# Column blocks of the mixer's input matrix in another order

## The reference, cut to what matters

```python
z = rms(x) @ w_in                     # 1024 x 2304: nine blocks of 256 columns
y_pool = pool_mix(z[:, 0:256])        # block 0: sums over 2, 4, 8, 16 tokens, then a small product
h = z[:, 256:512] * sigmoid(z[:, 512:768])          # blocks 1 and 2
y_conv = silu(layer_norm(depthwise_conv(h, 31))) @ pw_w + pw_b
q = rope(rms(z[:, 768:1280]) * g_q)   # blocks 3, 4: four heads of 128
k = rope(rms(z[:, 1280:1792]) * g_k)  # blocks 5, 6
v = z[:, 1792:2304]                   # blocks 7, 8
y_att = attention(q, k, v)            # prompt: causal; samples: two cached pages of keys and values each
x = x + concat(y_pool, y_conv, y_att) @ w_out
```

## Time and profile before

| | before |
|---|---|
| median of three runs | 1561.97 us |
| profiled execution | 1565.14 us |
| its span, first to last instruction | 1563.6 us |
| PE busy in the span | 1470.0 us (94%) |
| DVE busy in the span | 973.2 us (62%) |
| mean granted clock of TensorE | 0.972 |
| mixer stage, first layer | 137.8 us |
| mixer stage, second layer | 133.9 us |

### The profile page before, as it was taken

The page is one execution under the profiler, slowest core; times in us unless marked ns, Lnnn a source line. Parts: engine busy times, 40 slices in busy tenths (PEclk is TensorE's granted clock), DMA queues, the critical chain, the costliest instruction groups (busy, mean ns, idle before and its releaser), DMA issues. The chain is left out here.

```text
span 1563.6 us, 30270 instructions
## 1 busy us (share of the span) xinstructions
PE 1470.0 (94%) x11110; PEld 1386.0 (89%) x11110; DVE 973.2 (62%) x1366; ACT 594.1 (38%) x827; POOL 125.6 (8%) x167
## 2 busy tenths in 40 slices
PE   5999999968999999999989999997899998999998
PEld 4999999746978799999989999995688787999997
DVE  4766546886745467665466664578756554766643
ACT  4333344233534244333353333441445332433331
POOL 3000000342001110000000000006220110000000
PEclk7999999989999999999999999998999999999999
DMA  7566455326548647655456655552474666555552
GB/s 225 163 168 167 156 173 162 108 89 223 178 149 285 243 133 207 165 161 166 132 146 171 166 162 165 159 162 68 151 247 136 221 213 236 141 166 166 170 163 91
DMA packets 310010, 263.95 MB, mean 169 GB/s; under 512 B 7096, under 2 KB 292024, under 8 KB 309882
## 3 DMA queue, kind: packets, MB, share of 16 engines
q1 hardware_dynamic: 290242, 203.14, 43.3%
q0 software_dynamic: 13776, 48.97, 8.8%
q10 hardware_dynamic: 5896, 10.54, 2.2%
HBM read 254.65 MB, written 8.56 MB: 168 GB/s over the span
## 5 line engine op out<-in xcount | busy, mean ns | idle before, releaser
L1330 PE MATMUL pairs<-h_hi,w_hi 128*128 128x288 f32 x1824 | 545.5, 299 | 14.8 <-DVE h_lo L863 10.6
L1330 PE MATMUL pairs<-h_hi,w_lo 128*128 128x288 f32 x1824 | 544.2, 298 | 0.0
L1330 PE MATMUL pairs<-h_lo,w_hi 128*128 128x288 f32 x1824 | 543.9, 298 | 0.0
L860 DVE TENSOR_TENSOR w_lo<-raw_weights,w_hi 128x1024 fp32r<-128x1024 f32 (+1 forms) x388 | 450.3, 1202 | 135.9 <-ACT w_hi L637 132.8
L637 ACT ACTIVATE w_hi<-raw_weights 128x1024 fp32r<-128x1024 f32 (+1 forms) x388 | 382.0, 1033 | 282.6 <-PE pairs L1330 272.1
L1330 PEld LDWEIGHTS pairs<-h_hi,w_hi 128*128 128x128 f32 x1824 | 346.9, 190 | 20.0 <-DVE h_lo L863 11.2
L1330 PEld LDWEIGHTS pairs<-h_lo,w_hi 128*128 128x128 f32 x1824 | 347.7, 191 | 0.4
L1330 PEld LDWEIGHTS pairs<-h_hi,w_lo 128*128 128x128 f32 x1824 | 346.3, 190 | 0.0
L1330 PE MATMUL pairs<-g_hi,w_lo 128*128 128x288 f32 x704 | 208.7, 297 | 0.0
L1330 PE MATMUL pairs<-g_lo,w_hi 128*128 128x288 f32 x704 | 208.5, 296 | 0.0
L1330 PE MATMUL pairs<-g_hi,w_hi 128*128 128x288 f32 x704 | 207.4, 295 | 0.0
(11 more groups left out here) (266 smaller groups left out, 1527.3 us busy)
## 6 DMA issues: line engine op xcount, KB each, us to landing
raw_weights<-in_w_ffn_in SPq DMA_DIRECT2D x176, 512.0 KB
raw_weights<-in_w_ffn_out SPq DMA_DIRECT2D x32, 1024.0 KB
raw_weights<-in_w_in SPq DMA_DIRECT2D x18, 1024.0 KB
mem_kv<-in_cache_mem_k POOLq DMA_DIRECT2D x16, 1024.0 KB, 5.5
raw_weights<-in_w_ckv SPq DMA_DIRECT2D x16, 1024.0 KB
raw_weights<-in_w_ffn_out SPq DMA_DIRECT2D x16, 768.0 KB
raw_weights<-in_w_out SPq DMA_DIRECT2D x8, 1024.0 KB
raw_weights<-in_w_cq SPq DMA_DIRECT2D x8, 1024.0 KB
```

Source lines behind the costliest of these rows:

```text
L860: return dve.tensor_tensor(out, in0, in1, op)
L1330: return pe.matmul(out, lhsT, rhs, start=start, stop=stop, **kw)
```

## The change

The order of the nine units becomes q and k (blocks 3 to 6), convolution value and gate (1, 2), pooling (0), values (7, 8). On PE four units come first, then `qk_stat`, unit 4 (convolution value), `qk_root`, unit 5 (gate), the four rotary products, unit 6 (pooling), the two score pairs, unit 7, and only then the key transposes 0 and 1, which stood between the rotary products. On DVE the gating stands behind the rotary steps and the pooling input, just ahead of the scores. With it the taps move: none before the scores, then 2 in unit 7, 7 behind it, 5 in unit 8, and 17 behind the probabilities. ACT squares after units 0 to 3 and makes the sigmoid in its step 6. POOL gets one more wait: for `fresh_ready`, ahead of its convolution of the sample tokens. Two waits of DVE for freed key turns (lines 1076 and 1091) are left out, since those turns no longer lie between its own. The products and their number are the same.

```diff
--- before.py
+++ after.py
@@ -80,10 +80,10 @@
...
 CX_ORDER += ["ckv", "ckv", "mkt", "mkt", "ckv", "cx_s", "cx_s", "ckv", "cx_pt", "cx_pt", "cx_o", "cx_o", "cx_so"]
-MIX_ORDER = (["state_in"] + ["win"] * 6 + ["qk_stat", "win"] + ["qk_root"] * 4 + ["win"] + ["rope"] * 2 + ["att_k"] + ["rope"] * 2 + ["att_s", "att_k", "att_s"]
+MIX_ORDER = (["state_in"] + ["win"] * 4 + ["qk_stat", "win"] + ["qk_root"] * 4 + ["win"] + ["rope"] * 4 + ["win"] + ["att_s"] * 2 + ["win", "att_k", "att_k"]
              + ["att_k"] * 2 + ["win"] + ["att_k"] * 2 + ["att_pt"] * 2 + ["att_k"] * 2 + ["tok"] * 3 + ["pool", "state_out"]
              + ["att_o"] * 2 + ["pw", "att_so"])
-WIN_COLUMNS = (1, 2, 3, 4, 5, 6, 0, 7, 8)
+WIN_COLUMNS = (3, 4, 5, 6, 1, 2, 0, 7, 8)
 UNITS, TURNS = {}, {}
...
@@ -571,6 +571,8 @@
...
+                pool.wait_ge(fresh_ready, L + 1)
+                pool.sem_inc(pool_passed, 1)
                 for c in range(2):
...
@@ -739,13 +741,13 @@
...
                         norm_root(L, 1)
-                    if n == 2:
+                    if n == 6:
                         act.wait_ge(gate_in, L + 1)
                         act.activation(conv_gate[:, :, :], conv_gate[:, :, :], ACT.Sigmoid).then_inc(gate_ready, 1)
-                    if 3 <= n <= 6:
+                    if 1 <= n <= 4:
                         act.wait_ge(acc_free, passed(L, 0, TURNS["win"][n - 1]))
-                        act.activation(qk_squares[:, 2 * n - 6:2 * n - 4, :], z[:, 2 * n - 6:2 * n - 4, :], ACT.Square).then_inc(zsq_ready, 1)
-                    if n == 6:
+                        act.activation(qk_squares[:, 2 * n - 2:2 * n, :], z[:, 2 * n - 2:2 * n, :], ACT.Square).then_inc(zsq_ready, 1)
+                    if n == 4:
                         t = TURNS["qk_stat"][0]
...
@@ -1030,51 +1032,25 @@
...
-                free(scaled(conv_a[:, :, :], win(0)[:, :, 0:T]))
-                free(scaled(conv_gate[:, :, :], win(1)[:, :, 0:T]))
-                dve.drain()
-                dve.sem_inc(gate_in, 1)
-                free(scaled(z[:, 0:2, :], win(2)[:, :, 0:T]))
-                dve.wait_ge(gate_ready, L + 1)
-                tt(cxt[:, :, CBUF:CBUF + SEQ], conv_a[:, :, 0:SEQ], conv_gate[:, :, 0:SEQ], ALU.mult)
-                tt(fresh[:, 2:4, :], conv_a[:, :, SEQ:T], conv_gate[:, :, SEQ:T], ALU.mult)
-                dve.drain()
-                for c in range(2):
-                    last = dve.tensor_copy(conv_new(c)[:, :, CBUF:], fresh[:, 2 + c, :].rearrange("p (b t) -> p b t", b=SAMPLES))
-                last.then_inc(fresh_ready, 1)
-                for n in range(3, 6):
-                    free(scaled(z[:, 2 * n - 4:2 * n - 2, :], win(n, 3 * n - 9, 3 * n - 6)[:, :, 0:T]))
-                taps(9, 12)
+                for n in range(4):
+                    free(scaled(z[:, 2 * n:2 * n + 2, :], win(n)[:, :, 0:T]))
                 dve.wait_ge(rq_ready, L * 2 + 1)
...
-                pair = win(6)
-                tt(pxt[:, :, PBUF:PBUF + SEQ], pair[:, :, 0:SEQ], ap(norm_r, 0, [[0, 2], [1, SEQ]]), ALU.mult)
-                free(tt(fresh[:, 0:2, :], pair[:, :, SEQ:T], ap(norm_r, SEQ, [[0, 2], [1, TS]]), ALU.mult))
-                dve.drain()
-                for c in range(2):
-                    dve.tensor_copy(pool_new(c)[:, :, PBUF:], fresh[:, c, :].rearrange("p (b t) -> p b t", b=SAMPLES))
-                dve.drain()
-                dve.sem_inc(pool_in, 1)
+                free(scaled(conv_a[:, :, :], win(4)[:, :, 0:T]))
                 for j in range(4):
...
                     free(dve.drain())
-                    if j < 3:
-                        taps(12 + j, 13 + j)
-                free(scaled(v_t[:, 0:2, :], win(7, 15, 19)[:, :, 0:T]))
+                free(scaled(conv_gate[:, :, :], win(5)[:, :, 0:T]))
+                dve.drain()
+                dve.sem_inc(gate_in, 1)
                 for place, j in enumerate(ROPE_ORDER):
-                    if place == 2:
-                        dve.wait_ge(acc_free, passed(L, 0, TURNS["att_k"][0]))
-                        dve.sem_inc(dve_passed, 1)
                     pair = acc(L, TURNS["rope"][place])
...
@@ -1086,10 +1062,24 @@
...
+                pair = win(6)
+                tt(pxt[:, :, PBUF:PBUF + SEQ], pair[:, :, 0:SEQ], ap(norm_r, 0, [[0, 2], [1, SEQ]]), ALU.mult)
+                free(tt(fresh[:, 0:2, :], pair[:, :, SEQ:T], ap(norm_r, SEQ, [[0, 2], [1, TS]]), ALU.mult))
+                dve.drain()
+                for c in range(2):
+                    dve.tensor_copy(pool_new(c)[:, :, PBUF:], fresh[:, c, :].rearrange("p (b t) -> p b t", b=SAMPLES))
+                dve.drain()
+                dve.sem_inc(pool_in, 1)
+                dve.wait_ge(gate_ready, L + 1)
+                tt(cxt[:, :, CBUF:CBUF + SEQ], conv_a[:, :, 0:SEQ], conv_gate[:, :, 0:SEQ], ALU.mult)
+                tt(fresh[:, 2:4, :], conv_a[:, :, SEQ:T], conv_gate[:, :, SEQ:T], ALU.mult)
+                dve.drain()
+                for c in range(2):
+                    last = dve.tensor_copy(conv_new(c)[:, :, CBUF:], fresh[:, 2 + c, :].rearrange("p (b t) -> p b t", b=SAMPLES))
+                last.then_inc(fresh_ready, 1)
                 for j in range(2):
-                    if j == 1:
-                        dve.wait_ge(acc_free, passed(L, 0, TURNS["att_k"][1]))
-                        dve.sem_inc(dve_passed, 1)
                     pair = acc(L, TURNS["att_s"][j])
...
@@ -1104,15 +1094,16 @@
...
-                taps(19, 27)
-                free(scaled(v_t[:, 2:4, :], win(8)[:, :, 0:T]))
+                free(scaled(v_t[:, 0:2, :], win(7, 0, 2)[:, :, 0:T]))
+                taps(2, 9)
+                free(scaled(v_t[:, 2:4, :], win(8, 9, 14)[:, :, 0:T]))
                 normalise_probs(dve, L, p_exp, L * 16 + 8, probs, (slice(0, P), slice(P, 384)), p_probs)
...
                     free(dve.tensor_copy(probs_t[:, 2 * j:2 * j + 2, :], pair[:, :, 0:384]))
-                taps(27, CONV_K)
+                taps(14, CONV_K)
                 dve.sem_inc(conv_done, 1)
...
@@ -1452,7 +1443,7 @@
...
-                for n in range(6):
+                for n in range(4):
                     win(n)
...
@@ -1461,7 +1452,7 @@
...
                 ins.then_inc(acc_ready, 1)
-                win(6)
+                win(4)
...
@@ -1469,7 +1460,7 @@
...
                     ins.then_inc(acc_ready, 1)
-                win(7)
+                win(5)
...
@@ -1477,12 +1468,9 @@
...
                     ins.then_inc(acc_ready, 1)
-                    if place == 1:
-                        att_turned(0)
+                win(6)
                 for j in range(2):
-                    if j == 1:
-                        att_turned(1)
                     pair = take(L, TURNS["att_s"][j])
...
@@ -1490,6 +1478,9 @@
...
                     ins.then_inc(acc_ready, 1)
+                win(7)
+                att_turned(0)
+                att_turned(1)
                 pe.wait_ge(q_diag_ready, L * 2 + 1)
...
```

## The result

The changed kernel takes 1595.45 us (median of four runs, 1591.91 to 1596.3) against 1563.02 us for the kernel before in the same sessions: the ratio is 1.0208, with a 95% interval of 1.0186 to 1.0230. It is 32.4 us slower; 22 had been forecast. The profiled execution took 1596.3 us with a span of 1594.6 us, 31.0 more than before.

A forecast was written before the change was run, and what follows sets the result against it. DVE was taken to bound the mixer stage's second half. 11.9 + 8.1 (`sprobs` later in the two layers) + 2.6 (clock) - 0.5 (a wait gone) = 22.1 us on the median 1562.0 gave 1584 us, range 1565 to 1597.

The forecast's parts named there:

- The bound: Second half of the mixer stage: DVE sets the pace up to `sprobs` and PE follows.
- part 2: DVE from unit 6 to `sprobs`: 48.9 us with nothing held, 60.5 before; `sprobs` would start at 110.6.
- Part 1: Stage start to end of unit 6: early taps gone, PE well ahead, DVE takes unit 6 at 61.65 us.
- Part 3: POOL holds DVE's two-input instructions 12 us a layer; `sprobs` starts at 122.6, 11.9 and 8.1 us late.
- Part 4: The rest: one slow-clock spell of 2.6 us ahead of `sprobs` (bounds 0 to 10.4); four edits cost nothing.
- behind `sprobs`: After `sprobs` up to `wout`: same chain, 23.2 us, but a 0.53 us wait for token transposes goes in the second layer.
- second rival: Slower still: clock drops in both layers (10.4 us), POOL holds 15 us per layer; 36 us, 1598 us; chance 0.14.
- The first: Not slower: holding nearly vanishes as taps slip between POOL's steps; -4.5 us, 1557 us; chance 0.13.
- The third: PE's early lead to unit 8 counts if DVE has slack after unit 6; 16 us gain, 1546 us; chance 0.03.
- The waits that were named: New PE waits per layer, ended by DVE: about 8 us after unit 8, 10 before the last token transposes.
- The rule of tap 0 under POOL: Tap 0's two one-input instructions would be held under POOL's work too: 0.8 us a layer, sum 1.7 us higher.

## Why the prediction was right, and where it was not

**The bound and part 2: right. Part 1: right but for PE's clock.** DVE sets the pace from unit 6 to `sprobs`, and the 12 taps that lose their place among the early units are the largest term. With the room that DVE leaves ahead of unit 6 and the gating they were 13.3 us of the sum over both layers (110.6 unheld against 110.7 - 7.2 and 114.5 - 10.1). The run with the taps late in the old order costs 17 us in the timed runs, and the two runs with 12 taps left out put their place at 14 us (21 - 7).

**Part 3, holding: the size was near, the weight was not.** By the same reading as before, the held entries are too long by 10.2 us in the second layer (fresh 0.7, fourteen tap instructions 3.7, split 1.8, ten 4.1) and by 11.7 in the first, against 12 forecast: 4.6 us more than before. What was missed is what stands beside it: DVE waits 2.8 us for ACT's rounding in the second layer and 0.9 for unit 7, and up to 0.5 us at some other places. The sum had taken ACT as hidden. Residual in this stretch: 4.6 us, 3.9 of it in the second layer. The run with early rounding shows that holding and this wait cover for each other, and the two with POOL cut fit that, so neither is worth its row.

**Part 4, the clock: the step that failed.** I had read the spell of 1.2 GHz before as the effect of standstills in the root step, had put none into the new one, since there "the root step has almost no gap", and had let one spell of 2.6 us into the sum, for the gaps between the rotary steps. That one came, in unit 6 of the second layer, with 1.4 us. But the clock fell in the root step all the same, in both layers: unit 5 took 8.4 and 9.1 us, the root step itself 5.7 and 5.1 instead of 4.5, 3.1 us a layer. DVE starts on unit 6 at 65.0 and 66.4 instead of 61.65: 8.2 us in place of 2.6. These 5.6 us are the largest part of the 9.7 between the sum of 22.1 and the 31.8 found. The runs on 128 rows show that it was the products of the root step, not standstills. That this spell was free before and not now follows from the bound: before, DVE was behind PE at this place; now PE is behind DVE (DVE waits 5.64 us for unit 5 in the second layer, and 0.44 and 1.85 us for unit 6 in the two, where part 1 had "PE is well ahead here"). The old order on 128 rows bears that out: unit 7 at the full clock, and the same time (1.0006).

| term, both layers together | forecast | found |
|---|---|---|
| taps, gating and DVE's room ahead of unit 6 | 13.3 | 13.3 (taken over, not measured apart) |
| holding | 6.7 | 4.6 |
| clock and PE ahead of unit 6 | 2.6 | 8.2 |
| waits for ACT and PE behind unit 6 | 0 | 4.6 (what is left of the 30.7 by which `sprobs` is later) |
| behind `sprobs` | -0.5 | 1.1 |

The found column adds up to 31.8 us, the growth of the two stages; elsewhere the span is 0.8 us shorter. It must add up, as its fourth row is what the others leave.

**The number.** 1595.45 us lies above the 1571 to 1594 that the forecast gave itself and inside the range only by the margin kept for the second rival. With the bounds it names, 15 us of holding a layer and 10.4 of clock, the forecast's own end would have been 1598, the second rival's sum, and not 1594. That it came so near is in part luck: holding was put 2.1 us too high, while the clock, the waits and the stretch behind `sprobs` were 5.6, 4.6 and 1.6 us too low.

**The rivals.** The first (holding vanishes) fell: it grew. The second was right that the clock would be low in unit 5 of both layers and in unit 6 of one, though for unit 5 not by the rotary steps' gaps, and wrong on holding; its 1598 us is nearer than the 1584. The third failed as foreseen, and not for want of a lead: PE starts unit 8 at 88.4 us in the second layer, hardly sooner than before (88.8), but in the first at 86.2 in place of 94.4, and there too `sprobs` is 11.8 us later, for PE then stands still for DVE (7.9 us in the second layer). The waits that were named, 8 and 10 us, are there with 7.92 and 10.50. The sentence that DVE would be free of waits over 2 us did not hold (2.8 for ACT).

**Left open.** Why the stage behind `sprobs` takes 21.3 to 25.3 us from run to run of different kernels was not tested; it differs within one kernel between the layers (22.7 and 24.9 after), with PE at the lower clock for part of it. The rule of tap 0 under POOL, from the Trainium skill ("GPSIMD Engine Reference", 1. Specifications), has mixed rows: its two instructions take 1.49 us in the first layer, twice the usual 0.74, and 0.76 in the second, where POOL was in a long step of its own (1095.24 to 1098.58). The other kernels of the new order show the same, and with POOL cut they take 0.73 in the first layer too. The first layer bears out that DVE instructions with one SBUF input can be held too. By the rule the sum would have been 1.7 us higher; the rows show 0.75 us of that, in the first layer alone.

## What to carry to other kernels

When side work is woven into gaps, ask at which moment its input exists: moving the producer from the front to the middle of a stage makes the gaps ahead of it worthless, and the work piles up at the end, where nothing covers it. Count the cover, not the work: 12 taps were worth 7 us in one place and 21 in another. And ask of a clock spell, a held instruction or a late rounding whether it falls on the engine that is behind: the slow unit was free before, where DVE was behind, and a reorder that changes who is behind can put a price on it.

## What the runs showed of the hardware

- During products on 8 rows without a gap between them the granted clock fell from 1.0 to 0.5 (1.2 GHz), 2.8 and 3.7 us from the start of a step of 5.7 and 5.1 us; with products of the same columns on 128 rows, in the same place, it did not. It repeats in all kernels here that enter the step with the full clock (20 layers on 8 rows, 4 on 128).
- DVE's two-input instructions next to POOL's two-input ones took 0.73 us each in a run of 14 (10.28 us) and 0.88 in a run of 10 (8.82 us), against 0.47 undisturbed (34 in 16.16 us). A wait inserted or removed under POOL's work changes this: with 2.76 us of waiting gone, the instructions behind it were held 2.1 us longer.
- POOL's second pooling step started 3.94 us after its first had ended, in the second layer of either kernel, and 1.73 us in the first; with the sample convolution first, its second step came after the same 3.94 and 1.73 us, and with POOL cut after 3.96 and 1.75. What it is wasn't tested.
